# First output block kept transposed with its residual, second norm applied as a per-token factor at eviction

## What is computed

```python
# first block (swa): x is (512, 2048)
x = x + attention_1(rms_norm(x, norm1)) @ w_out1
# second block: h = 16 meta tokens, then x, 528 tokens
u = rms_norm_2(h, norm2)             # u = h * rsqrt(mean(h*h) + eps) * norm2, per token
proj = einsum('btd,de->bte', u, w_in2)   # 8 projections of 1024 columns
sb_q, sb_k, sb_v, sb_g, df_q, df_k, df_v, df_g = split(proj)
# per head: stick breaking on sb_*, differential softmax on df_* (own rms norm of
# q and k over 64 channels, rotary positions), each gated with silu(sb_g), silu(df_g)
y = concat(sb_out, df_out) @ w_out2
out = x + y
```

## Time and profile before

| | us |
|---|---|
| time, median of 3 runs (2076.12 to 2077.18) | 2076.85 |
| profiled execution: its own time | 2077.12 |
| profiled execution: span from first to last instruction | 2075.4 |
| TensorE busy | 1945.4 (94%) |
| VectorE busy | 880.9 (42%) |
| ScalarE busy | 858.9 (41%) |
| mean granted TensorE clock, share of full | 0.972 |

### The profile page before, as it was taken

One profiled execution on the slowest core, in us unless ns is written; L12 is line 12 of the kernel. 1 busy time (PEld: TensorE's weight loads), 2 busy tenths in 40 slices (PEclk: granted clock), 3 DMA queues, 4 the chain that ended last, 5 costly groups with the idle time before them and its releaser, 6 DMA issues.

```text
span 2075.4 us, 28753 instructions
## 1 busy us (share of the span) xinstructions
PE 1945.4 (94%) x9930; PEld 1562.0 (75%) x9930; DVE 880.9 (42%) x2215; ACT 858.9 (41%) x1915; POOL 31.6 (2%) x57
## 2 busy tenths in 40 slices
PE   4999998998998999499999999999999999988998
PEld 3777776776776877388878788887888888766886
DVE  4355555554555222333443434343343534434222
ACT  5455554454544222433524435353443535344221
POOL 1000000000000000000000000000000000000000
PEclk9999999999998999599999999999999999999999
DMA  6822322222213444322222222222222322203443
GB/s 153 203 76 72 87 72 67 71 66 71 66 46 82 121 121 128 97 66 78 64 63 82 63 74 70 69 72 63 81 63 63 81 62 69 74 20 110 123 121 111
DMA packets 311803, 173.37 MB, mean 84 GB/s; under 512 B 23552, under 2 KB 307232, under 8 KB 311216
## 3 DMA queue, kind: packets, MB, share of 16 engines
q1 hardware_dynamic: 306816, 158.89, 28.5%
q0 software_dynamic: 3904, 12.71, 2.3%
q10 hardware_dynamic: 1024, 1.07, 0.3%
HBM read 156.92 MB, written 14.66 MB: 83 GB/s over the span
## 4 chain that ended last, share of the span: by engine, by line
PE 68%; DMA 11%; DVE 9%; issue 5%; ACT 4%; SPq 1%; DVEq 0%; ACTq 0%
PE G L438 51%; DMA raw<-in_swa_w_out 4%; DMA raw<-in_w_out 4%; PE S L674 2%; DVE wl L1188 2%; ACT wh L811 1%; PE G L535 1%; DVE p L1257 1%; PE O L747 1%; PE S L719 1%; DVE p L1272 1%; DMA raw<-in_swa_w_in 1%; PE O L691 1%; PE G L522 1%; PE S L464 1%
## 5 line engine op out<-in xcount | busy, mean ns | idle before, releaser
L438 PE MATMUL G<-xh,wh 128*128 128x512 f32 (+1 forms) x2624 | 901.6, 375 | 14.4 <-DVE wl L1188 7.5
L438 PE MATMUL G<-xl,wh 128*128 128x512 f32 (+1 forms) x2624 | 847.5, 355 | 0.0
L438 PE MATMUL G<-xh,wl 128*128 128x512 f32 (+1 forms) x2624 | 843.8, 353 | 0.0
L1188 DVE TENSOR_TENSOR wl<-raw,wh 128x512 fp32r<-128x512 f32 x528 | 353.7, 689 | 841.2 <-ACT wh L811 830.3
L438 PEld LDWEIGHTS G<-xh,wh 128*128 128x128 f32 x2624 | 467.0, 190 | 119.3 <-issue 35.8
L438 PEld LDWEIGHTS G<-xh,wl 128*128 128x128 f32 x2624 | 463.3, 190 | 70.7
L438 PEld LDWEIGHTS G<-xl,wh 128*128 128x128 f32 x2624 | 464.2, 190 | 66.2 <-issue 7.0
L811 ACT ACTIVATE wh<-raw 128x512 fp32r<-128x512 f32 x528 | 313.5, 621 | 265.2 <-DMA raw<-in_swa_w_out 102.7
L1092 ACT ACTIVATE att<-att,st 128x144 f32<-128x144 f32 (+3 forms) x64 | 36.9, 576 | 184.1 <-DVE wmeta L1466 103.0
L907 ACT ACTIVATE p<-p,st 128x256 f32<-128x256 f32 (+1 forms) x128 | 60.8, 475 | 79.1 <-DVE st L1257 79.1
L464 PE MATMUL S<-mats,mixed 128*128 128x128 f32 x128 | 32.5, 430 | 53.4 <-DVE mixed L1198 21.3
(11 more groups left out here) (187 smaller groups left out, 1705.3 us busy)
## 6 DMA issues: line engine op xcount, KB each, us to landing
raw<-in_w_in SPq DMA_DIRECT2D x56, 1024.0 KB, 6.1
raw<-in_swa_w_in SPq DMA_DIRECT2D x32, 1024.0 KB, 5.4
raw<-in_swa_w_out SPq DMA_DIRECT2D x16, 1024.0 KB, 7.2
raw<-in_w_out SPq DMA_DIRECT2D x16, 1024.0 KB, 7.0
raw<-in_w_in POOLq DMA_DIRECT2D x8, 1024.0 KB, 7.4
rel_rows<-relb SPq DMA_DIRECT2D x1, 6128.0 KB, 35.8
mixed<-in_x SPq DMA_DIRECT2D x4, 1024.0 KB, 10.0
raw<-in_swa_w_in SPq DMA_DIRECT2D x8, 512.0 KB, 7.0
```

The source lines that it names most:

```text
L438: mm = pe.matmul(d, w[:, slot, k, :], v[:, k, a:b], start=(k == 0 and n == 0), stop=(k == KC - 1 and n == 2))
L1188: V.tensor_tensor(wl[:, slot, q, :], raw[:, slot, q, :], wh[:, slot, q, :].bitcast(F32), ALU.subtract).then_inc(w_lo, 1)
```

## The change

What it does:

- **First output block transposed.** The residual tile of `x` is transposed on TensorE (`x_transpose`, point 4 of the tile itself) and copied to a column buffer by ScalarE (`x_column`). When the tile's product is done, VectorE adds `G` and that buffer straight into `mixed[:, c, :]` (`x1_add`). The sum stays transposed, is stored to `x1` in 2 KB pieces, and ScalarE and VectorE form squares and their running sum per token (`x1_square`, `x1_squares`).
- **Second norm as a factor.** `xh`, `xl` are made from the unnormalised sum with the gain alone (`x1_hi`, `x1_lo`). One matmul with ones in the first head tile sums the squares over channels, ScalarE turns that into the factor `rs2` per token, and VectorE multiplies each of the 8 head tiles by it when it evicts it from PSUM (`scaled_out`), which takes these evictions from ScalarE. Rows, `row_sums(1)`, `scale_rows(1)` and the second `normalise` go.
- **Chunks split behind the last output tile.** Each product of tile 15 increments `chunk_free`; ScalarE and VectorE overwrite chunk c of `xh`, `xl` as soon as it was used for the last time.
- **Meta tokens, lambda and constants** are prepared inside output tiles 1 to 3; their loads go from SyncE to GpSimd, behind `a_out`.
- **Second output block.** VectorE adds the residual (now stored transposed) to `G`, TensorE transposes the sum at point 2 of the next tile, ScalarE copies it out for the store.
- **Windowed attention:** on VectorE `swa_scale` of block j-1 now stands ahead of `swa_bias` of block j.

```diff
@@ tensor
+            def x_transpose(c, half):
+                after(pe, r_in[half], 8 * (c - half) + 16)
+                after(pe, r_col, c)
+                src = chain_sq if half else chain_raw
+                for t in range(NB):
+                    mm = pe.transpose(T[:, P * t:P * t + P], src[:, P * t:P * t + P], ident)
+                mm.then_inc(r_t, 1)
+            def out1_tile(i, half, last=False):
...
+                after(pe, x1_sum, c - 1)
+                def at_point(p):
+                    if p == 4:
+                        x_transpose(c, half)
+                    if p == 6 and isinstance(c, int) and c == 2:
+                        meta_transpose()
...
-            normalise(KC)
@@ tensor, head(0), tile 0
+                        if isinstance(h, int) and h == 0 and ti == 0 and p == 6:
+                            pe.wait_ge(sq_sum, KC)
+                            pe.wait_ge(meta_f, 1)
+                            pe.matmul(O[:, :], ones, x1_sq[:, :], start=True, stop=True).then_inc(n2_stat, 1)
...
+                    if first:
+                        pe.wait_ge(x1_sum, KC - 1)
@@ scalar
+            def x1_hi(c):
+                act.wait_ge(chunk_free, c + 1) if c < KC - 1 else act.wait_ge(tile_done, T_OUT1 + KC)
+                act.wait_ge(x1_sum, c + 1)
+                A(xh[:, c, META:ALL], mixed[:, c, :], ACT.Copy, scale=gnorm[:, 1, c:c + 1]).then_inc(x_hi, 1)
...
+            out1_tile(KC // 2 - 1, 0)
+            x1_square(KC - 2, 0)
             for quarter in range(4):
                 split(T_HEAD // 2, 0, quarter, head_loaded(0, 0))
-            row_sums(1)
-            normalised_hi(1)
+                for c in range(3 * quarter, 3 * quarter + 3):
+                    x1_hi(c)
+                if quarter == 2:
+                    x_column(KC - 1, 1)
@@ scalar, finish, dfq and dfk
-                        for b, (a, e) in zip(two, ((0, TOK),) if ti == 0 else ((0, ALL // 2), (ALL // 2, ALL))):
-                            A(chain_raw[:, a:e], G[:, b, 0:e - a], ACT.Copy)
-                            last = A(chain_sq[:, a:e], G[:, b, 0:e - a], ACT.Square)
-                        last.then_inc(n_raw, 1)
+                        after(act, n_evict, count)
+                        width = ALL if ti else TOK
+                        A(chain_sq[:, 0:width], chain_raw[:, 0:width], ACT.Square).then_inc(n_raw, 1)
@@ vector, windowed attention
+                if m - 2 in SWA_S:
+                    swa_scale(u, SWA_S[m - 2])
                 if m in SWA_S:
                     swa_bias(i, u, g, SWA_S[m])
-                if m - 2 in SWA_S:
-                    swa_scale(u, SWA_S[m - 2])
@@ vector, transition and heads
+            for quarter in range(4):
+                split(T_HEAD // 2, 0, quarter)
+                if quarter == 0:
+                    x1_squares(KC - 2, 0)
+                for c in range(3 * quarter, 3 * quarter + 3):
+                    if c == 10:
+                        x1_add(KC - 1, 1)
+                    x1_lo(c)
+            for c in range(12, KC):
+                x1_lo(c)
+            x1_squares(KC - 1, 1)
+            def scaled_out(dst, two, s):
+                for b, (a, e) in zip(two, ((0, TOK),) if len(two) == 1 else ((0, ALL // 2), (ALL // 2, ALL))):
+                    at = META if len(two) == 1 else 0
+                    last = V.tensor_tensor(dst[:, a:e], G[:, b, 0:e - a], rs2[:, a + at:e + at], ALU.mult)
+                last.then_inc(s, 1)
...
+                    if p == 0:
+                        after(dve, tile_done, T_HEAD + 8 * h + ti + 1)
+                        after(dve, v_t, 2 * h)
+                        after(dve, used["dfq"] if ti else used["dfk"], h + ti)
+                        scaled_out(chain_raw, two, n_evict)
...
+                    V.tensor_tensor(gate[:, :], G[:, two[0], :], rs2[:, META:ALL], ALU.mult).then_inc(e_raw, 1)
                     after(dve, e_gate, 3 * n)
+                    V.tensor_tensor(gate[:, :], gate[:, :], gate_e[:, :], ALU.mult).then_inc(used[name], 1)
```

More of the change, by code:

```diff
@@ L433, in _, with product @@
         def _(pe):
-            def product(dst, slot, k, cols, last):
+            def product(dst, slot, k, cols, last, chunk_done):
                 for n, (w, v) in enumerate(((wh, xh), (wh, xl), (wl, xh))):
@@ new lines, in _ @@
+            act.wait_ge(tile_done, T_OUT1)
+            act.wait_ge(a_out, 8 * UNITS)
+            mixed_hi()
+            out1_tile(0, 0)
+            out1_tile(0, 1)
+            meta_sums()
+            meta_rstd()
+            out1_tile(1, 0)
+            second_constants()
+            out1_tile(1, 1)
+            meta_hi_part()
+            with act.Fori(2, KC // 2 - 1) as i:
+                for half in range(2):
+                    out1_tile(i, half)
+            out1_tile(KC // 2 - 1, 0)
@@ L1171, in _, with out2_copy, out2_tile @@
                 sb_step(N2 - 1, m)
-            def heads_over():
-                act.wait_ge(d_out, N2)
-                act.wait_ge(b_out, N2)
-            out_block(T_OUT2, KC, OUT2_LOADS, heads_over)
+            def out2_copy(c, i, half):
+                after(act, y_t, c + 1)
+                after(act, y_out[half], 16 * i)
+                A((gate_raw if half else gate_e)[:, :], T[:, :], ACT.Copy).then_inc(y_sum, 1)
+            def out2_tile(i, half, last=False):
+                if not last:
+                    for quarter in range(4):
+                        split(T_OUT2 // 2 + i + half, 1 - half, quarter, out_loaded(OUT2_LOADS, i + half, 1 - half))
+                if half:
+                    out2_copy(2 * i, i, 0)
+                elif not (isinstance(i, int) and i == 0):
+                    out2_copy(2 * i - 1, i - 1, 1)
+            act.wait_ge(tile_done, T_OUT2)
+            act.wait_ge(d_out, N2)
+            act.wait_ge(b_out, N2)
+            mixed_hi()
+            for half in range(2):
+                out2_tile(0, half)
+            with act.Fori(1, KC // 2 - 1) as i:
+                for half in range(2):
+                    out2_tile(i, half)
+            out2_tile(KC // 2 - 1, 0)
+            out2_tile(KC // 2 - 1, 1, last=True)
+            out2_copy(KC - 1, KC // 2 - 1, 1)
         @block.vector
@@ L1359, in tile @@
-                def tile(i, half, last=False):
-                    if not last:
-                        for quarter in range(4):
-                            split(first // 2 + i + half, 1 - half, quarter)
-                    if half:
-                        add(i, 0)
-                    elif not (isinstance(i, int) and i == 0):
-                        add(i - 1, 1)
-                for half in range(2):
-                    tile(0, half)
-                with dve.Fori(1, KC // 2 - 1) as i:
-                    for half in range(2):
-                        tile(i, half)
@@ new lines, in out1_tile, with meta_scale @@
+            def out1_tile(i, half):
+                c = 2 * i + half
+                for quarter in range(4):
+                    split(T_OUT1 // 2 + i + half, 1 - half, quarter)
+                if not (isinstance(c, int) and c == 0):
+                    x1_squares(c - 1, 1 - half)
+                x1_add(c, half)
+            def meta_scale():
+                dve.wait_ge(m_sq, 2)
+                V.tensor_tensor(ssq[0:META, 1, 2:3], ssq[0:META, 1, 0:1], ssq[0:META, 1, 1:2], ALU.add).then_inc(m_ssq, 1)
+                dve.wait_ge(m_rs, 1)
+                V.tensor_scalar(metar, metar, rstd[0:META, 1, 0:1], None, ALU.mult).then_inc(meta_rows, 1)
+                V.memset(rs2[:, 0:META], 1.0)
@@ L1540, in _, with y_add, out2_tile @@
                 sb_step(N2 - 1, m)
-            out_block(T_OUT2, KC)
+            mixed_lo(KC)
+            def y_add(c, i, half):
+                after(dve, tile_done, T_OUT2 + c + 1)
+                after(dve, y_in[half], 16 * (i + 1))
+                after(dve, y_t, c - 1)
+                V.tensor_tensor((chain_rs if half else y_col)[:, 0:TOK], G[:, half, :],
+                                (chain_sq if half else chain_raw)[:, 0:TOK], ALU.add).then_inc(y_raw, 1)
+            def out2_tile(i, half, last=False):
+                if not last:
+                    for quarter in range(4):
+                        split(T_OUT2 // 2 + i + half, 1 - half, quarter)
+                y_add(2 * i + half, i, half)
+            for half in range(2):
+                out2_tile(0, half)
+            with dve.Fori(1, KC // 2 - 1) as i:
+                for half in range(2):
+                    out2_tile(i, half)
+            out2_tile(KC // 2 - 1, 0)
+            out2_tile(KC // 2 - 1, 1, last=True)
 INPUTS = {"x": None, "rel_bias": None, "swa_norm": 0, "swa_w_in": 0, "swa_q_gain": 0, "swa_k_gain": 0, "swa_sinks": 0,
```

432 lines of the change are left out of this document (244 added, 188 removed).

## The result

The changed kernel takes 2013.92 us, the median of four runs (2011.41 to 2016.06), against 2077.01 before (2076.12 to 2082.62): a ratio of 0.9685, 95% interval 0.9666 to 0.9704. Its profiled execution took 2015.65 us with a span of 2014.0.

| stage | before | after | difference | forecast |
|---|---|---|---|---|
| start to the first scores | 120.24 | 119.31 | -0.9 | 0 |
| first scores to first output block | 522.79 | 511.40 | -11.4 | -5.8 |
| first output block to first head tile | 241.26 | 188.06 | -53.2 | -52.4 |
| heads and last stick-breaking part | 995.70 | 1004.15 | +8.4 | +7.5 |
| second output block to the end | 195.41 | 191.08 | -4.3 | -2.9 |

What follows compares the result with a forecast made beforehand. TensorE's own instructions were taken to bound the heads, with gains to be had elsewhere. Terms -46.9 - 9.3 + 7.7 + 0.7 - 5.8 = -53.6 against 2077.12 gave 2023.5, stated as 2023 us, range 2008 to 2036.

Steps and rivals of the forecast that it cites:

- Passage: From output tile 15 to the first head tile: the 46.9 us gap closes, all terms together -46.9 us.
- Rival A: Passage not seamless, through slower low parts or a queue stopping at its loop's end: 3 to 10 us more, chance 0.12.
- rival E: TensorE still stops behind output tile 15, running sum or last weights late: a full stop costs 20 us, chance 0.04.
- Pace of the output blocks: Output blocks: a round with one load in flight takes 12.6 us per tile, not 11.6; removing it gives -9.3 us.
- Heads: At the end of dfk, eviction behind later_l makes TensorE wait 1.1 us in each of 7 heads: +7.7 us.
- Rival B: In the heads, more evictions than dfk's are late: 8 to 14 us in all, chance 0.12.
- rival D: VectorE's queue becomes the pace of the heads, making the kernel slower than before, up to 2086 us; chance 0.02.
- The last gate: In the heads, no tile follows the last gate, so its extra multiply lies on the path: +0.7 us.
- Windowed attention: Swap of scaling and bias: steady units -2.6, two loop-round units -1.9, unit without tiles beside it -1.3; -5.8 us together.
- the ring: Windowed attention: maximum, exponents, copy, weight quarter, VectorE's split and scaling follow one another, 5.2 us a block.
- TensorE alone needs 4.8: Windowed attention: TensorE's own time from block 1 to 2, 5.13 less 0.33 us of wait.
- rival C: Windowed attention's swap pays in full: 1997 us at the most, 2003 to 2012 with half of it; chance 0.10.

Runs made afterwards that it cites:

- e5: Changed kernel, with TensorE waiting for all 16 low parts before the first product of the first head tile, not one per chunk: 2021.75 us, ratio 0.9718.
- e7: Kernel before, with VectorE's sum of tile c-2 ahead of the four weight splits of tile c in both output blocks: 2068.43 us, ratio 0.9935.
- e2: Kernel before, with only the windowed attention's swap added (VectorE scales a block ahead of the next bias and maximum): 2067.60 us, ratio 0.9932.
- e4: Changed kernel, with VectorE's weight splits in the windowed attention one step later: 1978.26 us, ratio 0.9505.
- e8: Kernel of e4, with VectorE's loop over the rounds of the windowed attention written out: 1969.44 us, ratio 0.9468.

## Why the prediction was right, point by point

The time lay in the range, 9 us under the forecast and just under the 2014 to which I had given the forecast's own spread. The sign of every term was right and the passage was by far the largest, as said; the windowed attention was to be the smallest of the four and came second.

- **Passage, right.** No gap: 0.23 us between the two products. VectorE made the low parts in 0.66 and not 0.70, ended them near 823.5 and not 825.4. Stage -53.2 for -52.4: the meta transposes cost 1.3 in tile 2 and not 0.9, and the block's first products ran 0.9 us less at half clock, which I had not counted. Rival A (3 to 10 us more) and rival E did not occur; e5 shows what a stop for all sixteen parts costs, 7.9 us.
- **Pace of the output blocks, right.** The round was the cause in both blocks (e7). The second block gave 3.2 in the distance of its evictions where I had said 2.9; another 0.8 lie in how long its first products ran at half clock, and 0.3 at its end, which I had not counted. That 2.9 came so close is partly luck of the one trace: in e2 the same block had 6.1 to lose.
- **Heads, right.** Stage +8.4 for +7.5; one more head with a stretch at the lower clock, 1.5 us, is the difference and more. I said 1.1 us for each of seven, the intervals between heads show 1.0 (0.83 listed and 0.16 of restart), and the place was the one named. VectorE's two halves took 0.77 together for my 0.80. I said ScalarE's relief could move `later_l` forward and took nothing for it; it did not move (1.00 us behind the start of the same stick-breaking product, before and after). Rival B (a second late eviction) and rival D did not occur: in the seven heads there is no other listed wait of TensorE at all. The last gate cost 1.2 and not 0.7: the first wait behind it grew from 3.76 to 4.58, by the length of an eviction and a hand-over, and the rest lies in the waits behind that one.
- **Windowed attention, wrong in size.** The term was -5.8 and came out at -11.4, close to the 12 that I had named as a sign of being wrong; this is most of what the forecast missed. The mechanism stands: block 0's wait goes, waits for `pT` appear, and the ring exists, in the order written down, at 5.07 and 5.00 us for my 5.2. Two terms of the sum were too small. First, the two units at a loop round were to gain 0.95 each and gained 2.2 (36.83 us where it was 39.06, and 36.58 where it was 38.78): 1.3 between the transposes of blocks 1 and 2, and 1.1 behind block 3, because the next unit's block 0 no longer waits. I had counted that gain in the steady units and left it out here. A longer stop takes 0.2 back. Second, each of the 13 steady units gained 0.4 and not 0.2: 1.07 instead of 0.98 behind block 3, 0.20 instead of 0.11 from block 0 to 1, and the ring took back 0.85, as forecast. The rest, the end included, gave 1.5 for 1.3.
- **"TensorE alone needs 4.8", wrong.** I had taken the distance of two transposes less the listed wait. TensorE's own distance is 4.58 (e4), since a listed wait understates what it costs. This does not change the swap's term, as the ring is longer than both, but it made rival C's far end too near: all waits of 16 units were to be worth 32 us, and e4, with both loop stops still in place, takes 48 off the stage of the kernel before. As to rival C itself, the 5.6 us that the swap gave beyond the forecast are half of the 11 to its nearer end, 2012.
- **PSUM sources.** The two evictions of 264 columns take 0.77 us together, and a sum of 512 columns takes 0.69 with one source in PSUM, as the weight split does with both in SBUF. The Trainium skill (VectorE: DVE Perf Modes, The TRN2 errata) gives a PSUM source a higher fixed cost on VectorE, by which the forecast would have had 0.9 us more; no row of this case shows that cost.

## What to carry to other kernels

A wait that the profile lists is less than what it costs: count the spacing of the instructions on both sides of it, not the idle time. But its removal brings that only if no other wait takes its place: the swap took away 0.98 us of listed wait in a unit and gained 0.4. In a queue that serves two consumers, ask of each instruction ahead of a late one whether it is wanted sooner; here three such moves (splits behind the scaling, low parts behind an eviction, a sum ahead of splits) brought 37, 7 and 10 us without a change in what is computed. When a stage follows another across a barrier, a wait per chunk can be worth more than an early start of the work; here it was 7.9 us against 2.6.

## What the runs showed of the hardware

VectorE's queue stood 4.5 to 5.2 us at each backward jump of its attention loop, and 1.3 to 1.7 us more within three instructions of that, in every trace with this loop; it did not stand at all when the loop was written out (e4 against e8).

TensorE at 1.2 GHz behind a stop of 4.85 us cost 2.9 us beyond the stop (e5). And in most heads it falls to that level without a stop: in the changed kernel it does so behind sixteen products of 16 columns, 2.2 us long. The same sixteen stand in every head, also in those where the clock stays at 1.00, so they alone do not decide it. First these products, then a window of the granted clock (0.63 over its two microseconds):

```profile
993.48 2.18 PE L701 MATMUL T<-dfk,dfq 64*128 64x16 f32 x16
```

```profile
996.00:998.00 2.00, 2.00 (x7) 1.17 (x6) 0.89 (x2) 0.00 (x0) 0.00 (x0) 0.63 0.00 0
```

A head with such a stretch is 1.5 us longer, in every kernel here, and which heads have one differs from run to run. Changes under 5 us in the heads can therefore be read from the intervals in a trace, but hardly from medians.
